# Low parts of six mLSTM weight units a layer made on GpSimd in pieces of 512 columns, in a two-layer fp32 encoder kernel

## The reference, cut to what matters

```python
u = x @ w_in
y_att = rms_norm(windowed_gqa(aq, ak, av, sink), att_g)
y_ml = mlstm_group(u[..., OFF_MQ:OFF_MV], u[..., OFF_MV:OFF_MO], u[..., OFF_MO:OFF_G], u[..., OFF_G:], ...)
return jnp.concatenate([y_att, y_ml], axis=-1) @ w_out
```

## Time and profile before

| | |
|---|---|
| three runs, us | 2223.54, 2217.67, 2218.72 (median 2218.72) |
| the profiled execution's own time, us | 2220.75 |
| its span, first to last instruction, us | 2219.1 |
| mean granted TensorE clock | 0.977 of full |
| instructions | 30120 |

### The profile page before, as it was taken

The page is one execution under the profiler, slowest core; times in us unless marked ns, Lnnn a source line. Parts: engine busy times, 40 slices in busy tenths (PEclk is TensorE's granted clock), DMA queues, the critical chain, the costliest instruction groups (busy, mean ns, idle before and its releaser), DMA issues.

```text
span 2219.1 us, 30120 instructions
## 1 busy us (share of the span) xinstructions
PE 2100.4 (95%) x10816; PEld 1670.5 (75%) x10816; DVE 1316.9 (59%) x2001; ACT 978.8 (44%) x1568; POOL 230.5 (10%) x268
## 2 busy tenths in 40 slices
PE   7989989999999899999898999999999989999997
PEld 6877767888878577777677886788888767777774
DVE  3875487822454765666877637782235476665557
ACT  3554565232422455555245557533333135555553
POOL 0000032000000321001100002300000032100004
PEclk9999999999998999999899999999999889999999
DMA  4154212321102699999511112033110059999995
GB/s 154 58 195 133 78 56 97 114 76 57 57 29 98 251 369 373 387 378 356 188 58 39 39 39 95 22 132 114 68 66 20 32 227 383 376 371 377 376 378 220
DMA packets 78526, 384.78 MB, mean 173 GB/s; under 512 B 10472, under 2 KB 11864, under 8 KB 43608
## 3 DMA queue, kind: packets, MB, share of 16 engines
q1 hardware_dynamic: 55264, 327.31, 38.9%
q0 software_dynamic: 10096, 30.38, 3.8%
q10 hardware_dynamic: 13064, 25.75, 3.1%
HBM read 352.27 MB, written 46.07 MB: 180 GB/s over the span
## 4 chain that ended last, share of the span: by engine, by line
PE 74%; DVE 14%; ACT 7%; issue 2%; DMA 1%; POOL 0%; DVEq 0%; ACTq 0%; POOLq 0%; SPq 0%
PE bank L2216 30%; PE bank L2736 10%; PE bank L2710 8%; PE bank L2700 8%; PE bank L2437 5%; DVE weight_slots_parts L1453 2%; PE bank L2547 2%; PE bank L2468 2%; PE bank L2237 1%; PE bank L2676 1%; ACT scratch L1075 1%; PE bank L2591 1%; PE bank L2607 1%; DVE scratch L1614 1%; ACT weight_slots_parts L973 1%
## 5 line engine op out<-in xcount | busy, mean ns | idle before, releaser
L1922 DVE TENSOR_TENSOR weight_slots_parts<-weight_slots,mixer_region_parts 128x2048 fp32r<-128x2048 f32 x140 | 321.6, 2317 | 85.1 <-ACT mixer_region_parts L1277 84.9
L2216 PE MATMUL bank<-weight_slots_parts,x_transposed_parts 128*128 128x512 f32 x864 | 281.4, 408 | 2.8 <-DVE weight_slots_parts L1453 2.8
L2216 PE MATMUL bank<-x_transposed_parts,weight_slots_parts 128*128 128x512 f32 (+1 forms) x1024 | 264.0, 345 | 7.2 <-DVE mixer_region L1566 4.0
L1277 ACT ACTIVATE mixer_region_parts<-weight_slots 128x2048 fp32r<-128x2048 f32 x140 | 260.9, 1908 | 22.1 <-ACT x_transposed L1352 18.1
L1453 DVE TENSOR_TENSOR weight_slots_parts<-weight_slots,weight_slots_parts 128x2048 fp32r<-128x2048 f32 x58 | 132.9, 2292 | 193.5 <-ACT weight_slots_parts L973 192.7
L2736 PE MATMUL bank<-weight_slots,x_transposed 128*128 128x512 f32 x560 | 247.6, 595 | 0.0
L2710 PE MATMUL bank<-mixer_region_parts,x_transposed_parts 128*128 128x256 f32 x1120 | 207.4, 283 | 0.2 <-DVE weight_slots_parts L1922 0.2
L2216 PEld LDWEIGHTS bank<-x_transposed_parts,weight_slots_parts 128*128 128x128 f32 x1024 | 180.6, 193 | 29.8 <-DVE mixer_region L1566 5.3
L2700 PE MATMUL bank<-mixer_region_parts,x_transposed_parts 128*128 128x512 f32 x560 | 192.1, 414 | 5.1 <-ACTq L1317 2.3
L2736 PEld LDWEIGHTS bank<-weight_slots,x_transposed 128*128 128x128 f32 x560 | 104.0, 191 | 118.6 <-issue 103.0
L2216 PEld LDWEIGHTS bank<-weight_slots_parts,x_transposed_parts 128*128 128x128 f32 x864 | 163.6, 195 | 36.6 <-DVE weight_slots_parts L1453 4.5
(11 more groups left out here) (319 smaller groups left out, 3524.2 us busy)
## 6 DMA issues: line engine op xcount, KB each, us to landing
weight_slots<-in_w_gate SPq DMA_DIRECT2D x70, 1024.0 KB, 7.2
weight_slots<-in_w_up SPq DMA_DIRECT2D x70, 1024.0 KB, 7.0
weight_slots<-in_w_down SPq DMA_DIRECT2D x70, 1024.0 KB, 7.5
weight_slots<-in_w_in SPq DMA_DIRECT2D x20, 1024.0 KB, 5.0
slots_y<-x_transposed ACTq DMA_DIRECT2D x66, 256.0 KB, 7.2
weight_slots<-in_wkv_mem SPq DMA_DIRECT2D x16, 1024.0 KB, 4.8
slots_y<-in_consts SPq DMA_DIRECT2D x6, 2304.0 KB, 17.7
weight_slots<-in_w_out SPq DMA_DIRECT2D x8, 1024.0 KB, 5.2
```

Of the source, the lines that this page charges most:

```text
L1277: nc.scalar.activation(hi, raw, ACT.Copy).then_inc(moe.high_ready, 1)
L1922: v.tensor_tensor(lo, raw, hi.bitcast(F32), ALU.subtract).then_inc(moe.low_ready, 1)
L2216: ins = pe.matmul(ps, lhs[i](k), rhs[j](k), start=k == 0 and a == 0, stop=k == KD - 1 and a == 2)
```

## The change

For mq0, mq1, mv0, mv1, mo0 and mo1 of both layers VectorE's subtraction of 128x2048 is taken out. GpSimd makes them behind its `memset` of the ones, each as four subtractions of 128x512, after waiting for the unit's high part and for the low part that comes before it in the order. VectorE's remaining low parts get a wait for the one before them, which may now be GpSimd's, and the wait behind them counts by the order.

```diff
+POOL_LOW = ("mq0", "mq1", "mv0", "mv1", "mo0", "mo1")
...
-        def half_raw(name):
+        def half_raw(name, k=KD):
             s = slot_of(name) * 4096
-            return by_k(ring[:, s + 2048:s + 4096])
+            return by_k(ring[:, s + 2048:s + 4096], k)
...
                     nc.gpsimd.memset(va[:, :, :, MD:MD + 1], 1.0).then_inc(ones_made, 1)
+                    for name in POOL_LOW:
+                        pool.wait_ge(w_hi, len(SPLITS) * l + SPLITS[name] + 1)
+                        pool.wait_ge(w_lo, len(SPLITS) * l + SPLITS[name])
+                        lo, raw, hi = half_lo(name, 4), half_raw(name, 4), half_hi(name, 4).bitcast(F32)
+                        for k in range(4):
+                            ins = nc.gpsimd.tensor_tensor(lo[:, k, :], raw[:, k, :], hi[:, k, :], ALU.subtract)
+                        ins.then_inc(w_lo, 1)
...
                         else:
+                            dve.wait_ge(w_lo, len(SPLITS) * now[0] + SPLITS[name])
                             v.tensor_tensor(half_lo(name), half_raw(name), half_hi(name).bitcast(F32), ALU.subtract).then_inc(w_lo, 1)
-                        own(w_lo)
+                        dve.wait_ge(w_lo, len(SPLITS) * now[0] + SPLITS[name] + 1)
...
-                            if STREAM[i - 1] in SPLIT_BEHIND:
+                            if STREAM[i - 1] in SPLIT_BEHIND and SPLIT_BEHIND[STREAM[i - 1]] not in POOL_LOW:
                                 low_weights(SPLIT_BEHIND[STREAM[i - 1]])
```

## The result

| | before | after |
|---|---|---|
| median, us | 2219.91 (16 runs, 2214.99 to 2229.7) | 2233.9 (16 runs, 2227.01 to 2241.33) |
| profiled execution, us | 2220.75 | 2239.07 |
| its span, us | 2219.1 | 2237.1 |
| mean granted TensorE clock | 0.977 | 0.973 |

The changed kernel is slower: the ratio is 1.006, with a 95% interval from 1.0046 to 1.0073. That is +14.0 us between the medians and +18.3 us between the two profiled executions. The 16 executions of either kernel spread over some 15 us, so a few microseconds between two of them mean nothing by themselves.

A forecast was written before the change was run, and what follows sets the result against it. TensorE, busy 95% of the span, was taken as the bound, through its in-order waits. Lateness +10.0, clock +4.8 and relief 0 made +14.8 us on 2218.7, so 2233.5 us (+0.67%), range 2223 to 2241.

The forecast's parts named there:

- The price of a unit: On GpSimd: four 128x512 subtractions at 1.18 us each, 4.8 us a unit with gaps; bounds 4.2 and 5.6 us.
- mv1 and mo1, on the critical path: TensorE needs these weights at once, so restarts 2.5 us later, twice a layer: +10.0 us, bounds 7.6 and 13.2.
- lateness: At mv1 and mo1: TensorE's restart moves from 2.4 to 4.9 us after the high part, +10.0 us in all.
- The clock after the longer pauses: Behind TensorE's pauses at mv1 and mo1: half-clock spells of 1.65 us after three of four, +4.8 us.
- VectorE's relief: VectorE's queue behind mq0 and mv0 moves up, at most -2.7 us a layer; blocking by GpSimd offsets it, taken as 0.
- holds: Behind mq0 and mv0: three VectorE operations blocked by GpSimd, together up to 2.9 us against 2.3 us saved.
- mq1 and mo0, nothing: Low parts of these units are covered by TensorE's work, so taking them off VectorE is worth nothing.
- Faster by VectorE's queue: Rival: VectorE's queue ahead of TensorE's restarts holds the stream; eight low parts return 18.4 us, giving 2200; chance 0.04.
- The small loss: Rival: VectorE's relief comes whole (-5.4 us), clock holds in most pauses; +1 to +6.5 us, inside noise; chance 0.17.

The follow-up runs named there:

- e8: e2 with each GpSimd unit cut into 16 operations of 128 columns instead of four of 512; median 2212.66 us, ratio 0.9962 to the kernel before.
- e3: The changed kernel with 12 matmuls whose result nobody reads put into each of TensorE's four pauses; median 2227.38 us, ratio 1.0041 to the kernel before.
- e1: The changed kernel with only mv1 and mo1 on GpSimd, the other four units back on VectorE; median 2240.68 us, ratio 1.0101 to the kernel before.
- e2: The changed kernel with only mq0, mq1, mv0 and mo0 on GpSimd, mv1 and mo1 on VectorE; median 2220.93 us, ratio 1.0006 to the kernel before.
- e9: The kernel of e1 run again unchanged in another batch; median 2237.69 us, ratio 1.0086 to the kernel before.
- e5: e2 with GpSimd at mq0 and mv0 also waiting for VectorE's next row maxima; median 2213.45 us, ratio 0.9969 to the kernel before.
- e4: The kernel before, with TensorE using the low part last in the first tile of mv1 and mo1; median 2211.46 us, ratio 0.997.
- e7: e2 with each GpSimd unit as one operation of 2048 columns; median 2220.11 us, ratio 0.999 to the kernel before.
- e10: The changed kernel with TensorE using the low part last in the first tile of mv1 and mo1; median 2225.22 us, ratio 1.0028 to the kernel before.

## Why the prediction was right

The forecast was 2233.5 us, that is +14.8 us; the medians gave +14.0 us and 2233.9 us. The profiled execution, forecast at 2235.5 us, took 2239.07. By its steps:

- **The price of a unit.** Taken as 4.8 us, measured 4.96 us where GpSimd runs alone (1.26 to 1.29 us an operation instead of 1.18), 5.1 to 5.6 us beside VectorE. That is 0.1 us an operation over half of the 1024-column add. The fixed part of an operation accounts for it: 0.46 us for 128 columns (e8) and 1.29 for 512 lie on a line that leaves 0.18 us for none, and halving the add counted half of that. Nothing shows the fp32r output to cost anything.
- **mv1 and mo1, on the critical path, +10.0 us.** TensorE waited 13.0 us in place of 2.8, so +10.2 us; e3, where only the lateness is left, puts it at 10.9 us. Shown by e1 and e2: these two units carry the loss, the other four none to speak of.
- **The clock after the longer pauses, +4.8 us.** I took three of four pauses at 1.65 us; all four lost it, at 1.42 us over the 12 matmuls behind each: 5.7 us. Both factors were off, in opposite directions. e3's stretches give the 5.7 us back. How many spells come is partly luck: e1 and e9 had three of four, as I had taken it.
- **VectorE's relief, 0 us.** Behind mq0 it was 2.33 us saved and 2.55 us held, 0.35 us less than the 2.9 us that I had allowed at worst. e2's stretch grew by 1.8 us, of which 1.3 us is the step that kernels without this edit have too; the 0.5 us left and the median within noise agree with 0. e5 and e8 show the cause, each with the holds taken away in its own way.
- **mq1 and mo0, nothing.** Nobody waited for GpSimd at mq1, mo0, mq0 or mv0, as said.
- **The rivals.** Faster by VectorE's queue fell at the point named for it: TensorE's restart followed GpSimd at once. The small loss needed relief without holds, and they came. The relief exists, however, and e8 got it.

By parts the stretches grew by 8.2 + 8.4 = 16.6 us at mv1 and mo1, which is 10.9 us of lateness by e3 and 5.7 us of clock, and by 1.1 us ahead of them, 0.9 us of it the step in layer 1. The mechanism and the sizes of its terms were right: lateness was low by 0.2 to 0.9 us, the clock by 0.9 us, and relief less holds near the 0 that I took. That the forecast met the median within 0.8 us is luck: the traces add up to some 17.6 us, and the median lies 3.6 us under them. Most medians of the table stand 2 to 5 us from their stretches, and about as far as single executions of one kernel are from their median; no trace exists of those other executions, so where the difference lies isn't shown. Runs of this kind settle a mechanism by its stretch, cut finely enough to see where a step stands, and the median only to a few microseconds.

One reading of the prediction was off and changed nothing: GpSimd's first affine select, at 277.90, comes 40 us after mo1's high part (its low part starts at 237.87), not 35.

Several numbers of the expectations missed. e1 and e9 lost more by their medians than the 12 to 17 us that I had expected. e4 and e5 gained more, by medians that their own stretches don't carry. e7's delay of 0.9 us was 0.15 us. e8's units were longer and its relief larger. And e10 kept more of the loss than the 4 us that I had allowed.

## What to carry to other kernels

Before an elementwise step goes to a slower engine, ask of each unit how long after its producer the consumer takes it. Where that slack was over the slower duration, the move cost next to nothing here (mq0, mq1, mv0, mo0); where it is zero, the whole difference is paid, and the matmuls behind the pause may be paid at half clock on top. Where GpSimd works beside VectorE's operations on SBUF, cut its work into small pieces even if the sum gets longer, and use a late operand in the last matmuls of its tile, not in the first.

## What was not expected of the hardware

- The cut of GpSimd's work has a small fixed price: 0.46 us for 128 columns, 1.29 for 512 and 4.70 for 2048, so a unit is 7.35, 5 and 4.7 us. But VectorE got in between two GpSimd operations: no hold behind mq0 was longer than one of them. That made the slowest cut the best one.
- A VectorE operation with a single input in SBUF was held too (L1580, in e7 L1579: 0.29 us alone, 2.98 us in e7). The prediction had put it at risk with no row of such a hold; now there are several. Operations with an input in PSUM kept their 0.48 us.
- A pause of 3.1 to 3.5 us in dense TensorE work was followed by a half-clock spell 10 times out of 12 (four of four in the changed kernel, three of four each in e1 and e9), and the 12 matmuls behind it took some 4.4 us or more instead of 3.0. Single pauses of 0.5 to 0.9 us and of 1.4 to 1.6 us (e10) were not. Twelve matmuls whose result nobody reads, in that pause, kept the clock.
